# Column groups of the input projection in the order f, q, pool, g, v, with the sample state read before its decay

## What is computed

```python
proj = h @ w_in                                   # 1024 -> 5 x 512
q, fx, ix, g, u = split(proj)                     # four groups of HGRN2, and the pooling input u
f = lb + (1.0 - lb) * sigmoid(fx)
o, S = hgrn2_scan(silu(q), log(f), 1.0 - f, ix)   # S_t = diag(f_t) S_{t-1} + k_t v_t^T ; o_t = S_t^T q_t
o = o * rsqrt(mean(o * o) + EPS) * hg_norm * silu(g)
yp, new_buf = multiscale_pool(u, buf, ...)        # trailing means over 2, 4, 8, 16 tokens, then a linear map
x = x + concat(o, yp) @ w_o
x = x + ffn(rmsnorm(x))                           # layer 0 dense, layer 1 a top-2-of-8 mixture
```

## Time and profile before

| | us |
|---|---|
| median of three runs | 959.97 |
| the profiled execution | 959.26 |
| its span in the profile | 957.5 |
| TensorE busy (matmul) | 909.5 (95%) |
| VectorE, ScalarE, GpSimd busy | 696.7, 574.7, 172.8 |
| mean granted TensorE clock | 0.963 |

### The profile page before, as it was taken

One profiled execution on the slowest core, in us unless ns is written; L12 is line 12 of the kernel. 1 busy time (PEld: TensorE's weight loads), 2 busy tenths in 40 slices (PEclk: granted clock), 3 DMA queues, 4 the chain that ended last, 5 costly groups with the idle time before them and its releaser, 6 DMA issues.

```text
span 957.5 us, 15159 instructions
## 1 busy us (share of the span) xinstructions
PE 909.5 (95%) x5838; PEld 835.8 (87%) x5838; DVE 696.7 (73%) x802; ACT 574.7 (60%) x709; POOL 172.8 (18%) x147
## 2 busy tenths in 40 slices
PE   6989999999999999799978998999999999999996
PEld 6989899999999999798968997888888888888885
DVE  5799574766665547984545568989898989898964
ACT  6654476545543346544552566868686868686852
POOL 4174166222221121730640000000000000000001
PEclk9999799999999999997985899999999999999998
DMA  8833035655695435320342349999999999999921
GB/s 310 291 117 111 1 111 215 213 178 176 201 323 183 150 120 188 131 88 1 122 176 89 130 155 412 413 331 389 338 393 335 389 337 390 337 398 327 391 92 46
DMA packets 51767, 217.82 MB, mean 228 GB/s; under 512 B 6097, under 2 KB 6225, under 8 KB 51311
## 3 DMA queue, kind: packets, MB, share of 16 engines
q1 hardware_dynamic: 50670, 210.15, 60.1%
q0 software_dynamic: 608, 5.27, 1.5%
q10 hardware_dynamic: 432, 1.64, 0.4%
HBM read 210.06 MB, written 7.43 MB: 227 GB/s over the span
## 4 chain that ended last, share of the span: by engine, by line
PE 80%; DVE 5%; DMA 4%; ACT 4%; POOL 3%; issue 3%; SPq 1%; DVEq 0%; POOLq 0%; ACTq 0%
PE bank L1578 38%; PE bank L1300 9%; PE bank L1301 9%; PE bank L1302 9%; PE bank L1552 3%; PE bank L1329 2%; PE bank L1448 2%; PE bank L1370 2%; DMA sb_raw<-in_in_units_dram 2%; PE bank L1627 1%; ACT sb_w_hi L505 1%; DMA h_saved<-at_scaled_m 1%; POOL at_state L468 1%; DVE at_sided L952 1%; PE bank L1587 1%
## 5 line engine op out<-in xcount | busy, mean ns | idle before, releaser
L860 DVE TENSOR_TENSOR sb_w_lo<-sb_raw,sb_w_hi 128x1024 fp32r<-128x1024 f32 (+1 forms) x116 | 164.8, 1421 | 73.1 <-ACT sb_w_hi L505 70.9
L1300 PE MATMUL bank<-at_act_hi,sb_w_hi 128*128 128x264 f32 x672 | 193.8, 288 | 12.2 <-DVE sb_w_lo L860 9.4
L505 ACT ACTIVATE sb_w_hi<-sb_raw 128x1024 fp32r<-128x1024 f32 (+1 forms) x116 | 127.0, 1100 | 128.7 <-PE bank L1302 112.8
L1578 PE MATMUL bank<-sb_w_hi,at_packed 128*128 128x512 f32 (+1 forms) x768 | 193.9, 382 | 4.0 <-DVE sb_w_lo L1078 2.6
L1302 PE MATMUL bank<-at_act_hi,sb_w_lo 128*128 128x264 f32 x672 | 191.4, 285 | 0.0
L1301 PE MATMUL bank<-at_act_lo,sb_w_hi 128*128 128x264 f32 x672 | 191.3, 285 | 0.0
L1078 DVE TENSOR_TENSOR sb_w_lo<-at_raw_e,sb_w_hi 128x1408 fp32r<-128x1408 f32 (+1 forms) x112 | 159.1, 1446 | 30.4 <-ACT sb_w_hi L728 30.2
L1578 PEld LDWEIGHTS bank<-sb_w_hi,at_packed 128*128 128x128 f32 x768 | 141.9, 191 | 28.5 <-DVE sb_w_lo L1078 2.3
L728 ACT ACTIVATE sb_w_hi<-at_raw_e 128x1408 fp32r<-128x1408 f32 (+1 forms) x112 | 139.3, 1244 | 44.0 <-PE bank L1578 37.2
L1078 DVE TENSOR_TENSOR sb_w_lo<-sb_raw,sb_w_hi 128x1408 fp32r<-128x1408 f32 (+1 forms) x104 | 149.7, 1470 | 21.2 <-ACT sb_w_hi L728 20.5
L728 ACT ACTIVATE sb_w_hi<-sb_raw 128x1408 fp32r<-128x1408 f32 (+1 forms) x104 | 130.5, 1262 | 37.5 <-PE bank L1578 35.9
(11 more groups left out here) (253 smaller groups left out, 1457.3 us busy)
## 6 DMA issues: line engine op xcount, KB each, us to landing
sb_raw<-in_moe_w_up_dram SPq DMA_DIRECT2D x36, 704.0 KB, 7.1
at_raw_e<-in_moe_w_down_dram SPq DMA_DIRECT2D x49, 512.0 KB, 6.4
at_raw_e<-in_moe_w_gate_dram SPq DMA_DIRECT2D x35, 704.0 KB, 8.9
sb_raw<-in_up_units_dram SPq DMA_DIRECT2D x44, 512.0 KB, 3.3
sb_raw<-in_moe_w_gate_dram SPq DMA_DIRECT2D x29, 704.0 KB, 8.5
sb_raw<-in_in_units_dram SPq DMA_DIRECT2D x39, 512.0 KB, 3.5
sb_raw<-in_moe_w_down_dram SPq DMA_DIRECT2D x39, 512.0 KB, 5.2
at_raw_e<-in_moe_w_up_dram SPq DMA_DIRECT2D x28, 704.0 KB, 6.1
```

The lines of the kernel that those rows point to most:

```text
L505: act.activation(w_hi[s][:, 0:kts, :], raw[s][:, 0:kts, :], ACT.Copy).then_inc(hi_done, 1)
L860: dve.tensor_tensor(w_lo[s][:, 0:kts, :], raw[s][:, 0:kts, :], w_hi[s][:, 0:kts, :].bitcast(f32), ALU.subtract).then_inc(lo_done, 1)
L1300: pe.matmul(out[:, 0:T], w_hi[s][:, k, :], hi[:, c, :], start=(c == 0), stop=False)
L1578: mm = pe.matmul(bank[first_bank + p][:, 0:width], s, w[:, c0:c0 + width], start=(k == 0 and n == 0), stop=(k == last and n == 2))
```

## The change

The five column groups come in the order f, q, pool, g, v. Everything on f (its sigmoid, `logf`, the scan L960, `keys`) moves to steps (1, 0) to (1, 3), q's gate to (2, 0), levels -1 to 7 to the steps behind u9 to u17, the pool's windows to steps (4, 0) to (4, 3), the sum over the past pool rows (`sum_past`) behind u8. The sample state is read undecayed: `sample_qf` is q times f, and the 32 small matmuls go behind u12 and u16. The sums are copied to SBUF (`sample_sums`, `past_sums`). The spreads of v are gone: v of the samples is turned (`v_rows`), written to a DRAM tensor by GpSimd's queue and read back into all partitions at once (`v_all`, 2 MB). Four states are decayed by GpSimd ahead of the output pass, four by ScalarE in it. `scaled_m`, `h_lo` and `token_hot` lie elsewhere, and the wait for `h_out` moves from VectorE (ahead of `token_hot`) to ScalarE.

```diff
-GROUPS = (0, 1, 3, 2, 4)
+GROUPS = (1, 0, 4, 3, 2)
...
-        scaled_m = at("scaled_m", [128, KT, T], 95744)
-        h_lo = at("h_lo", [128, 3, D_MODEL], 104192, f32r)
-        token_hot = at("token_hot", [128, 3, N_EXPERTS, CAP], 91904, f32r)
+        h_hi = at("h_hi", [128, 3, D_MODEL], 80000, f32r)
+        scaled_m = at("scaled_m", [128, KT, T], 71552)
+        h_lo = at("h_lo", [128, 3, D_MODEL], 92288, f32r)
+        token_hot = at("token_hot", [128, 3, N_EXPERTS, CAP], 104576, f32r)
...
-                def decay_state(h):
-                    gp.wait_ge(state_in, 64 * (L + 1))
-                    fs = proj[:, 1, h, SEQ:T].unsqueeze(2).broadcast_to([128, DEC, 128])
-                    gp.tensor_tensor(state[:, :, h, :], state[:, :, h, :], fs, ALU.mult).then_inc(state_decayed, 1)
...
-                    if 2 <= j < 5:
-                        decay_state(j - 1)
...
+                gp.wait_ge(rows_copied, L + 1)
+                gp.dma_start(v_saved[ds(L, 1), :], v_rows[:, :]).then_inc(v_out, 16)
+                gp.wait_ge(v_out, 16 * (L + 1))
+                gp.wait_ge(scored, 17 * (L + 1))
+                gp.wait_ge(kdec_done, 2 * (L + 1))
+                gp.dma_start(v_all[:, :, :, :].rearrange("p b h v -> p (b h v)"), v_saved[ds(L, 1), :].broadcast_to([128, DEC * HG_WIDTH])).then_inc(v_in, 16)
...
+                for b in range(DEC // 2):
+                    fs = proj[:, 1, :, SEQ + b:SEQ + b + 1].broadcast_to([128, HEADS, 128])
+                    gp.tensor_tensor(state[:, b, :, :], state[:, b, :, :], fs, ALU.mult).then_inc(early_decayed, 1)
...
+                def update_state(b):
+                    gp.wait_ge(outer_done, 8 * L + b + 1)
+                    if b < DEC // 2:
+                        gp.wait_ge(early_decayed, 4 * L + b + 1)
+                    else:
+                        gp.wait_ge(late_decayed, 4 * L + b - 3)
+                    gp.tensor_tensor(state[:, b, :, :], v_all[:, b, :, :], state[:, b, :, :], ALU.add).then_inc(state_done, 1)
...
+                for kt, bs in enumerate(((0, 1), (2,), (3,), (4,), (5, 6), (7,), (), ())):
+                    square_tile(version, out, kt)
+                    for b in bs:
+                        update_state(b)
...
                     if (it, s) == (1, 0):
                         act.wait_ge(bank_read, IN0[L] + 4)
-                        act.activation(sig[:, :, :], proj[:, 0, :, :], ACT.Sigmoid).then_inc(sig_done, 1)
+                        act.activation(proj[:, 1, :, :], proj[:, 1, :, :], ACT.Sigmoid).then_inc(sig_done, 1)
+                        act.preload_act_table(ACT.Ln)
+                    if (it, s) == (1, 2):
+                        act.wait_ge(forget_done, 4 * (L + 1))
+                        act.activation(logf[:, :, :], proj[:, 1, :, 0:SEQ], ACT.Ln).then_inc(logf_done, 1)
+                        act.preload_act_table(ACT.Sigmoid)
...
+                        act.activation(sig[:, :, :], proj[:, 0, :, :], ACT.Sigmoid).then_inc(sig_done, 1)
                         act.preload_act_table(ACT.Exp)
                     if (it, s) in ACT_LEVELS:
                         exp_level(ACT_LEVELS[(it, s)])
...
+                    if (it, s) == (2, 2):
+                        act.wait_ge(past_summed, L + 1)
+                        act.activation(past_sums[:, :, :], bank[7][:, 0:4 * DEC].rearrange("p (g b) -> p g b", g=4), ACT.Copy).then_inc(past_copied, 1)
+                    if (it, s) == (4, 0):
+                        put(12)
+                        put(13)
+                    if (it, s) == (4, 1):
+                        act.wait_ge(sampled, 5 * (L + 1))
+                        act.activation(sample_sums[:, :, :, :].rearrange("p a h b -> p (a h b)"), bank[2][:, SIDE.start:BESIDE.stop], ACT.Copy).then_inc(sums_copied, 1)
+                        put(14)
+                        put(15)
+                        act.wait_ge(end_diff, L + 1)
+                        act.activation(diff[0][:, :, SEG:SEQ], diff[0][:, :, SEG:SEQ], ACT.Exp, scale=-1.0).then_inc(end_exp, 1)
+                        act.activation(diff[0][:, :, 0:1], decay[:, :, SEQ - 1:SEQ], ACT.Exp).then_inc(end_exp, 1)
+                        act.preload_act_table(ACT.Sigmoid)
+                    if (it, s) == (4, 2):
+                        put(16)
+                        act.wait_ge(bank_read, IN0[L] + 16)
+                        act.wait_ge(q_gated, L + 1)
+                        act.activation(sig[:, :, :], proj[:, 3, :, :], ACT.Sigmoid).then_inc(sig_done, 1)
+                        act.preload_act_table(ACT.Ln)
...
+                    act.wait_ge(v_in, 16 * (L + 1))
...
+                        done = act.activation(v_all[:, b, h, :], v_all[:, b, h, :], ACT.Copy, scale=keys[:, h, SEQ + b:SEQ + b + 1])
...
+                STATE_STEPS = (((4,), ()), ((5,), ()), ((), (0, 1)), ((), (2, 3)), ((), (4, 5)), ((6,), (6,)), ((7,), (7,)), ((), ()))
...
+                def decay_state(b):
+                    for h in range(HEADS):
+                        done = act.activation(state[:, b, h, :], state[:, b, h, :], ACT.Copy, scale=proj[:, 1, h, SEQ + b:SEQ + b + 1])
+                    done.then_inc(late_decayed, 1)
...
+                    if (it, s) == (1, 1):
+                        dve.wait_ge(lb_step, 11)
                         dve.wait_ge(sig_done, 3 * L + 1)
-                        dve.wait_ge(bank_read, IN0[L] + 4)
-                        dve.tensor_tensor(proj[:, 0, :, :], proj[:, 0, :, :], sig[:, :, :], ALU.mult).then_inc(q_gated, 1)
...
                         for h in range(HEADS):
                             dve.tensor_scalar(proj[:, 1, h, :], proj[:, 1, h, :], lspan[:, L, h:h + 1], lbound[:, L, h:h + 1],
                                               ALU.mult, ALU.add).then_inc(forget_done, 1)
...
+                    if (it, s) == (1, 3):
...
                         dve.tensor_tensor_scan(decay[:, :, :].rearrange("p h t -> p (h t)"), segments[:, :, :].rearrange("p h t -> p (h t)"),
                                                logf[:, :, :].rearrange("p h t -> p (h t)"), 0.0, ALU.mult, ALU.add).then_inc(decay_done, 1)
...
+                    if (it, s) == (2, 0):
+                        dve.wait_ge(sig_done, 3 * L + 2)
+                        dve.wait_ge(bank_read, IN0[L] + 8)
+                        dve.tensor_tensor(proj[:, 0, :, :], proj[:, 0, :, :], sig[:, :, :], ALU.mult).then_inc(q_gated, 1)
...
+                        dve.tensor_tensor(sample_qf[:, :, :], proj[:, 0, :, SEQ:T], proj[:, 1, :, SEQ:T], ALU.mult).then_inc(qf_done, 1)
...
-            dve.wait_ge(h_out, 16)
-            dve.wait_ge(h_turned, 6)
...
-                def spread(b):
-                    if b >= 2:
-                        pe.wait_ge(outer_done, 8 * L + b - 1)
-                    for h in range(HEADS):
-                        mm = pe.matmul(bank[4 + b % 2][:, 128 * h:128 * (h + 1)], v[:, h, SEQ + b:SEQ + b + 1].broadcast_to([128, 128]), ident,
-                                       start=True, stop=True)
-                    mm.then_inc(v_spread, 1)
...
+                PE_LEVELS = {(2, 1): -1, (2, 2): 0, (2, 3): 1, (3, 0): 2, (3, 1): 3, (3, 2): 4, (3, 3): 5, (4, 0): 6, (4, 1): 7}
...
+                SAMPLE_HEADS = {(3, 0): (0, 1), (4, 0): (2, 3)}
...
                 def between(it, s):
+                    if (it, s) == (2, 0):
+                        sum_past()
+                    if (it, s) in SAMPLE_HEADS:
+                        pe.wait_ge(bank_read, IN0[L] + 4 * (it - 1) + 3)
+                        for h in SAMPLE_HEADS[(it, s)]:
+                            sample_head(h)
+                    if (it, s) == (4, 0):
+                        pe.wait_ge(kq_done, L + 1)
+                        pe.matmul(bank[2][:, BESIDE], ones, sample_kq[:, :, :].rearrange("p h b -> p (h b)"), start=True, stop=True).then_inc(sampled, 1)
                     if (it, s) in PE_LEVELS:
                         score_level(PE_LEVELS[(it, s)])
+                    if (it, s) == (4, 1):
+                        pe.wait_ge(sums_copied, L + 1)
+                def sum_past():
...
+                    pe.wait_ge(bank_read, IN0[L] + 8)
...
+                        mm = pe.matmul(bank[7][:, DEC * g:DEC * (g + 1)], pool_past[:, 128 * g:128 * (g + 1)], pick[0:rows, g, :], start=True, stop=True)
...
+                def map_pool(g):
+                    w = (win_a, win_b)[g % 2]
+                    pe.wait_ge(pooled, 4 * L + g + 1)
+                    pe.wait_ge(bank_read, IN0[L] + 16 + g + 1)
+                    pe.matmul(bank[g][:, 0:T], pool_w[:, g, :], w[:, g, PAD:], start=True, stop=True).then_inc(pool_mapped, 1)
+                map_pool(0)
+                map_pool(1)
...
                     out_part(s, range(HEADS, 2 * HEADS))
+                    if s == 0:
+                        sum_heads(0)
+                    if s == 1:
+                        sum_heads(1)
+                        pe.wait_ge(hgo_scaled, 16 * L + 8)
```

(1 more changed line is left out.)

285 lines of the change are left out of this document (128 added, 157 removed).

## The result

The changed kernel takes 955.37 us (median of 15 runs, 950.05 to 956.31) against 962.49 for the kernel before (15 runs on the same chip, 955.56 to 968.55). The ratio is 0.992, 95% interval 0.9903 to 0.9937. So it is faster, by 0.8%: 7.1 us where 13.4 were forecast, and 8.8 us above the 946.6 of the forecast. The profiled execution took 955.17 us (span 953.3; before 957.5), so the two spans differ by 4.2 us only: the profiled execution before lay 3.2 us under its median. The changed kernel's 15 runs fall in groups, eleven of 954.7 to 956.3 us (the profiled one among them), three of 950.1 to 950.3 and one of 952.5.

What follows compares the result with a forecast made beforehand. It took TensorE as busy nearly throughout the dense FFN, with losses at `sided` waits, half-clock tails and GpSimd's squares. Terms 3.4 + 4.5 + 6.2 - 4.4 - 0.5 + 3.5 = 12.7 off 959.3 gave 946.6 us, range 938 to 957.

Steps and rivals of the forecast that it cites:

- the clock behind the heads: Input passes: half clock behind pairs of sample heads after u12 and u16, 1.7 us in 0.65 of four pairs, 4.4 lost.
- Decays out of the input pass: Input passes: `sided` no longer held up by GpSimd's decay of the state; losses of 6.9 and 5.8 us removed.
- f first: Input passes: new waits at `sum_past` (5.8, 1.3 us) and level 0 (1.1 each); with the decays' gains, net 0 and 3.4.
- the second rival: The forecast's second alternative: longer waits and half clock after stalls, 954.5 us, range 951 to 960, chance 0.27.
- Out of the tail: Tails behind the input passes: half clock and idle time won back, less 2.5 us of new costs; 4.5 and 6.2 gained.
- The paragraph on the rule of the Trainium skill: Low activity puts TensorE at 1.2 GHz; if so behind all four pairs, 10 us lost instead of 4.4, sum 952.2.
- Spreads out of layer 0's output pass: ScalarE sets the end, GpSimd's squares covered; 0.5 us lost (bound +0.4 to -3). E: end of the first output unit.
- Layer 1's output pass: GpSimd's squares end and the root starts earlier, 4.6 us; `token_hot` saves 1.35, half clock costs 2.4: 3.5 gained.
- v by transfer: `v_all` lands at about T + 15 (T: input pass end), first used at T + 23.7: slack 8.7 us, no cost.
- waits eat the gain: Rival: longer f chain, 5.8 us waits in both layers (4.5 more), half clock twice 1.7; 954.5 us, chance 0.27.
- The clock holds: Rival: two sample heads do not lower the clock; 940.4 us, range 937 to 942, chance 0.15.
- The slower one, by a late `v_in`: Rival: output passes grow as ScalarE waits for a transfer landing after 16 us; 965 to 975 us, chance 0.08.

Runs made afterwards that it cites:

- e5: The kernel before, with its four GpSimd decays of the state per layer cut to 2 elements each (state left undecayed): 951.09 us, ratio 0.989.
- e6: The changed kernel, with layer 0's load of the sample state behind the weights of u8 to u11: 950.23 us, ratio 0.990 to the kernel before.
- e1: The changed kernel, with single sample heads behind u11, u13, u15 and u16 instead of pairs behind u12 and u16: 945.46 us, ratio 0.983 to the kernel before.
- e12: The changed kernel, with the score level between the two heads of each pair instead of behind them: 945.52 us, ratio 0.984 to the kernel before.
- e4: The changed kernel, with GpSimd's state additions in layer 1 placed later, the last three behind the last square: 948.62 us, ratio 0.985 to the kernel before.
- e3: The changed kernel, with the 32 products of v and k per output pass on VectorE instead of ScalarE: 963.55 us, ratio 1.002 to the kernel before.
- e7: The changed kernel, with all eight state decays on GpSimd ahead of the output pass, none on ScalarE: 958.22 us, ratio 0.997 to the kernel before.

## Why the prediction went wrong

The sign was right and most of the mechanisms named were the ones at work; the size was not, 13.4 us against 7.1. The step that failed most is the clock behind the heads, mis-sized at 4.4 us where 10.3 were lost; next comes the half clock behind the new stall, which the sum put at nothing and which took 3.1. The missing 13.6 us in four stretches were in the profiles partly covered by the experts' 5 us, which is luck. Point by point, in its order:

**Decays out of the input pass.** Right: the `sided` instructions take 0.68 to 0.69 us on all levels of the changed kernel; e5 shows 6.0 and 5.3 us for the 6.9 and 5.8 of the sum.

```profile
L1020 DVE TENSOR_TENSOR at_sided<-at_diff,at_keys x16: 680/685/687, 53.6 to 427.6; 128x512 f32<-128x512 f32 x16
```

**f first.** The waits were right, 5.5 us for 5.8 and 1.4 for 1.3, and so was the chain, link by link: the read of u7 that ends it was done at 44.3, for 44.4. Of the 5.5 us the late weights are 2.4 (e6), the rest is the chain itself. Level -1 waited 1.6 us in layer 1 and level 0 nowhere, for 1.1 in each. Left out of the sum, without a reason, was what the stall does to the clock: 3.1 us lost behind it in layer 0. It stood only in the second rival, as 1.7.

**Out of the tail.** The new tails, with the first output unit, take 18.7 us in each layer; the sum had 17.8 and 17.6, though the wait for `mix_lo` was shorter than forecast, 1.4 for 2.0. The rest is in small pieces that no run separates.

**Clock behind the heads.** This is the step that failed. The sum took 4.4 us, as 0.65 of the four pairs at 1.7 us each; measured are 10.3 us in four of four, and e1 gives 9.9. That the clock falls behind a pair was no chance of 0.65 but came every time. The price per pair, from 3.4 us at half clock that no row showed, was right behind u16 (1.7 and 1.8 us lost) and half of what came behind u12 (3.4 in each layer). Behind u12 the second head already ends at half clock and it holds through the level and into the unit; behind u16 both heads run at full clock (3.63 us) and only then it falls (0.58 over 94.5 to 97.7). The earlier trace rows were misread: "four in a row ended at half clock" were four heads with levels 6 and 7 and part of the attention between them, so the evidence was stronger than it was taken for. The paragraph on the rule of the Trainium skill gave the right total, 10 us, though as 2.5 for each pair, which none of them lost. The lesson of e12 was nowhere in the prediction: the same work, with a level between, costs nothing there.

**Spreads out of layer 0's output pass.** Right that ScalarE and not TensorE sets the end: `norm_lo` at E + 27.7 for E + 26.2, idle time 9.6 us for 7.7. Half clock for the whole next unit cost 2.5 us where 0.9 were taken, again with a half clock of 3.4 us that no row showed. GpSimd was not covered as forecast either: its squares ended at E + 32.4 (158.9), not E + 29.8. The 23.1 us behind its first product are not the 24.96 less one square that the text calls them (its squares took 0.6 to 1.6 us), and 25.3 came. +2.9 instead of +0.5, within the bound of 3.

**Layer 1's output pass.** Wrong in its size: GpSimd's squares ended at E + 29.7, not E + 27.5, and the root started at E + 31.1, not E + 28.0. The forecast gave no sum for its E + 27.5. GpSimd had no gap from its first addition at E + 6.2 on; its squares took 1.5 us more than the same ones before, nearly all of it in one, 2.21 us instead of 0.75, beside a split of VectorE that starts with it:

```profile
483.73 2.21 POOL L415 TENSOR_TENSOR at_square_m<-at_square_m 128x264 f32<-128x264 f32 x1
```

Behind the idle time the sum of squares took 1.2 us at half clock. The term that failed is GpSimd's queue, and e4 shows what lay in its order, 6.8 us. From the root to the experts 0.6 us were saved where the forecast had 1.05 lost (1.35 less 2.4), so the whole stretch is only 1.3 us off.

**v by transfer.** Right. It was issued at 115.8 and took 8.1 us (7.4 forecast), so it ended at T + 16.1, and ScalarE's first product started at T + 24.4 without a wait:

```profile
at_v_all<-v_saved POOLq DMA_DIRECT2D x1, 2048.0 KB, 8.1
```

**Of the rivals**, "waits eat the gain" has the right number, 954.5 us against 955.4, but mostly by luck. Of its 7.9 us, the 4.5 for layer 1's wait did not come (1.4 us, as in the likeliest case), and the half clock behind the stalls came in layer 0 alone; the loss was mostly behind the heads and in the output passes. "The clock holds" was the opposite of what happened. The slower one, by a late `v_in`, had no part.

## What to carry to other kernels

Price a group of tiny matmuls by what the clock does behind it, not by its own length: two heads of 1.8 us cost 1.7 to 3.4 us more behind them, and the same two between full units, with 1.8 us of full-width matmuls between them, cost nothing. Look at what else of that kind stands near: in the old tail, heads with levels between them still met half clock. When an engine is relieved, sum up the queue of each of the others in the same stretch before the gain is booked; here ScalarE and GpSimd had both hardly a gap and VectorE was slowed by GpSimd, and moving work between them (e3, e7) made the kernel slower, while a new order in one queue (e4) gave 7 us. Where a chain waits for a transfer, look at what stands behind the large transfer as well: moving it by two units only made other weights late.

## What the runs showed of the hardware that was not expected

- Two sample heads in a row (3.5 us of one-column matmuls) brought the granted clock to 0.72 to 0.85 over the 11 to 12.5 us around them, four times of four; single ones in the input pass, with a level or a unit between them, left it at 1.00 (e1, e12). In the tail of the kernel before, with small matmuls ahead of them, heads with levels between them ran at 0.62 and less from the third on in layer 0. The Trainium skill (TensorE: Matmul & The Clock Gate, Part 1) has the fall after low activity; here it came with TensorE busy all the time (12.50 of 12.50 us).
- The same wait of 1.4 us for the past sums in layer 1 was followed by a clock of 1.00 in the changed kernel and of 0.66 in e1 and e12 (374 to 379 us).
- A VectorE product with one large input in SBUF took 0.28 us in a gap of GpSimd and beside it 0.46 in the median, up to 1.34 (e3).
- The experts' stretch of the same code took 447.2 to 447.6 us in ten profiles and 450.9 and 451.6 in two, with clocks of 0.76 and 0.65 to 0.66 over its first 40 us.
